# Three rounded passes for the scores and values of a memory attention, on pairs of token tiles

## What is computed

```python
def cross_attn(h, k, v, w_xq, w_xo):
    b, t, _ = h.shape
    q = (h @ w_xq).reshape(b, t, MEM_HEADS, MEM_HD)
    s = jnp.einsum('bthd,bmhd->bhtm', q, k).astype(jnp.float32) * (MEM_HD ** -0.5)
    p = jax.nn.softmax(s, axis=-1).astype(v.dtype)
    o = jnp.einsum('bhtm,bmhd->bthd', p, v).reshape(b, t, D_MODEL)
    return o @ w_xo
```

## Time and profile before

| | us |
|---|---|
| median of 3 runs | 2224.11 |
| lowest and highest run | 2221.91, 2224.35 |
| the profiled execution | 2224.57 |
| its span in the profile | 2222.8 |
| PE busy | 2191.7 |
| DVE busy | 1372.6 |
| ACT busy | 684.4 |

### The profile page before, as it was taken

How to read it: one execution, slowest core, us unless ns; L and a number is a source line. 1 busy time by engine, 2 the same in 40 slices (tenths; PEclk the granted TensorE clock), 3 DMA queues, 4 the chain that set the end, 5 groups by cost and what they waited for, 6 DMA issues and landing times.

```text
span 2222.8 us, 40929 instructions
## 1 busy us (share of the span) xinstructions
PE 2191.7 (99%) x15968; PEld 2137.3 (96%) x15968; DVE 1372.6 (62%) x2564; ACT 684.4 (31%) x1124; POOL 327.4 (15%) x335
## 2 busy tenths in 40 slices
PE   8999999999999999999999999999999999999998
PEld 7999999999999999987899988999999999999998
DVE  6865555646667765466868335258765555466665
ACT  6332232222123332246714034124323222221124
POOL 2010100123221000024400000000111010133230
PEclk9999999999999999999999999999999999999999
DMA  7231231243323221057623334422223123153222
GB/s 235 68 110 57 69 102 57 90 170 112 106 77 129 72 59 40 21 175 245 209 91 118 132 114 142 146 93 76 88 63 110 57 76 96 58 208 114 78 77 79
DMA packets 222577, 234.37 MB, mean 105 GB/s; under 512 B 8979, under 2 KB 179745, under 8 KB 222201
## 3 DMA queue, kind: packets, MB, share of 16 engines
q1 hardware_dynamic: 222465, 232.83, 32.3%
HBM read 180.42 MB, written 52.48 MB: 105 GB/s over the span
## 4 chain that ended last, share of the span: by engine, by line
PE 61%; DVE 2%; ACT 1%; DMA 1%; issue 0%; SPq 0%; DVEq 0%; ACTq 0%
PE bank L3018 18%; PE bank L3020 17%; PE bank L3019 17%; PE bank L3685 1%; PE bank L3697 1%; PE bank L3717 1%; PE bank L3578 0%; PE bank L3574 0%; PE bank L3584 0%; PE bank L3706 0%; PE bank L3739 0%; DMA w_raw<-in_w_out_dram 0%; DMA out_mem_k_prompt_dram<-kst 0%; PE bank L3727 0%; ACT dec L1658 0%
## 5 line engine op out<-in xcount | busy, mean ns | idle before, releaser
L3018 PE MATMUL bank<-h_hi,w_hi 128*128 128x352 f32 (+1 forms) x3392 | 1048.5, 309 | 1.7 <-DVE h_lo L2912 1.1
L3020 PE MATMUL bank<-h_hi,w_lo 128*128 128x352 f32 (+1 forms) x3392 | 1040.3, 307 | 0.0
L3019 PE MATMUL bank<-h_lo,w_hi 128*128 128x352 f32 (+1 forms) x3392 | 1040.0, 307 | 0.0
L3018 PEld LDWEIGHTS bank<-h_hi,w_hi 128*128 128x128 f32 x3392 | 636.8, 188 | 4.3 <-DVE h_lo L2912 1.4
L3019 PEld LDWEIGHTS bank<-h_lo,w_hi 128*128 128x128 f32 x3392 | 637.9, 188 | 0.0
L3020 PEld LDWEIGHTS bank<-h_hi,w_lo 128*128 128x128 f32 x3392 | 636.8, 188 | 0.0
L2208 DVE SCALAR_TENSOR_TENSOR x<-bank,x 128x352 f32<-128x352 f32 x448 | 226.8, 520 | 129.7 <-PE bank L3020 128.8
L3019 PE MATMUL bank<-xr,w_hi 128*128 128x264 f32 x640 | 181.8, 284 | 0.0
L3018 PE MATMUL bank<-xr,w_hi 128*128 128x264 f32 x640 | 181.4, 283 | 0.1
L3020 PE MATMUL bank<-xr,w_lo 128*128 128x264 f32 x640 | 181.5, 284 | 0.0
L1944 DVE TENSOR_TENSOR w_lo<-w_raw,w_hi 128x1024 fp32r<-128x1024 f32 x120 | 144.4, 1218 | 23.5 <-ACT w_hi L1264 23.5
(11 more groups left out here) (431 smaller groups left out, 2850.5 us busy)
## 6 DMA issues: line engine op xcount, KB each, us to landing
act_keep<-act SPq DMA_DIRECT2D x88, 264.0 KB, 2.0
w_raw<-in_w_gate_dram SPq DMA_DIRECT2D x44, 512.0 KB, 5.1
w_raw<-in_w_up_dram SPq DMA_DIRECT2D x44, 512.0 KB, 3.9
w_raw<-in_w_down_dram SPq DMA_DIRECT2D x44, 512.0 KB, 3.6
h_raw<-act_keep SPq DMA_DIRECT2D x24, 528.0 KB, 4.5
l_raw<-act_keep SPq DMA_DIRECT2D x20, 528.0 KB, 5.4
w_raw<-in_w_in_dram SPq DMA_DIRECT2D x18, 512.0 KB, 4.4
x<-x_keep SPq DMA_DIRECT2D x6, 1408.0 KB, 10.5
```

The source lines that it names most:

```text
L3018: eng.matmul(out, a_hi, b_hi, start=first, stop=False, skip_group_check=onto)
L3019: eng.matmul(out, a_hi, b_lo, start=False, stop=False, skip_group_check=onto)
L3020: return eng.matmul(out, a_lo, b_hi, start=False, stop=last, skip_group_check=onto)
```

## The change

In the attention, scores and values become three rounded passes, and an item becomes a **unit** u of one head and two token tiles (16 units; the heads of a pair of tiles come in the order 0, 3, 1, 2).

- **Splits.** ACT makes the high parts of `q` (into `h_hi`), of `kT` and of `v`, DVE the low parts: tiles 0 to 4 of `q`, `kT` and `v` around the last `evict_q`, tiles 5 to 7 in the units 2, 4 and 6. PE's first scores wait for the low part of `kT`.
- **Scores** of a unit: 2 tiles x 2 blocks x 3 passes of 256 columns, 12 matmuls in place of 8 exact ones. **Values**: 2 x 2 x 3 passes of 256 columns, 12 in place of 8 exact ones of 128 columns over 2 tiles.
- **Turned weights** of a unit fill bank 4 (512 columns): ACT takes the high part and DVE the low part (`att_turned`), where DVE made one copy.
- **Sample keys.** All four groups of sequence b stand in unit b. ACT copies groups 0, 1 and 2, DVE group 3 (`take_key`), as the last of its operations of the unit except a split; `sample_scores(b)` waits for it (`kt_copied`).
- **Sample values** come two to a unit, in units 11 to 14.
- **Weights.** The third and fourth unit of `w_xo` are split after the last values (the slots hold `kT_hi` and `v_hi` until then). `w_split(U_XO + 2)` stands on DVE between the last low part and the low part of the sample rows. The loads of units 4 and 5 of `w_xo` move behind the reload of `x`.

```diff
-            for group in range(2):
-                hi_pair(U_XQ + 4 + 4 * group)
-                hi_pair(U_XQ + 6 + 4 * group)
...
+            for pair in range(3):
+                hi_pair(U_XQ + 4 + 2 * pair)
...
+            for t in range(5):
+                q_hi(t)
+            eng.wait_ge(p_ready, 100)
+            eng.wait_ge(s_rows, 48)
+            eng.activation(kT_hi[:, :, :], kT[:, :, :], ACT.Copy).then_inc(n_hi, 1)
+            eng.activation(v_hi[:, :, :], v[:, :, :], ACT.Copy).then_inc(n_hi, 1)
...
+                if nq == 22:
+                    q_lo(4)
+                    row_lo("k", kT_lo, kT, kT_hi)
+            row_lo("v", v_lo, v, v_hi)
...
             att_exp(0)
+            att_turned(0)
             att_exp(1)
...
+            for u in range(NU):
+                if u < NB:
+                    take_key(u, 0)
+                    take_key(u, 1)
+                if u + 2 < NU:
+                    att_exp(u + 2)
+                if u >= 1:
+                    att_o(u - 1)
+                if u + 1 < NU:
+                    att_turned(u + 1)
+                if u < NB:
+                    take_key(u, 2)
+                if u in (2, 4, 6):
+                    q_hi(4 + u // 2)
...
+            for u in range(NU):
+                if u + 2 < NU:
+                    att_max(u + 2)
+                if u == S_SOFT:
+                    sample_max()
+                if u >= 1:
+                    att_lo(u - 1)
+                if u + 2 < NU:
+                    att_scale(u + 2)
+                if u + 1 < NU:
+                    att_turned(u + 1)
+                if u < NB:
+                    take_key(u)
...
+            att_lo(NU - 1)
+            w_split(U_XO + 2)
+            eng.wait_ge(a_oh, NU + 1)
...
+            w_split(U_XO + 3)
...
+                        mm = three(o, h_hi[:, a, tk], h_lo[:, a, tk], kT_hi[:, 2 * h + kd, :], kT_lo[:, 2 * h + kd, :],
+                                   kd == 0, kd == 1)
...
+                        mm = three(o, v_hi[:, m, c_:c_ + P], v_lo[:, m, c_:c_ + P], pT_hi[u % 2][:, m, :], pT_lo[u % 2][:, m, :],
+                                   m == 0, m == 1)
...
-                eng.wait_ge(b_ta, 4 * b + 4)
+                eng.wait_ge(b_ta, 3 * b + 3)
+                eng.wait_ge(kt_copied, 4 + b + 1)
...
+            for u in range(NU):
+                if u + 2 < NU:
+                    scores(u + 2)
+                if u < NB:
+                    sample_turn(u, 0)
+                    sample_turn(u, 1)
+                if u + 1 < NU:
+                    turn_p(u + 1)
+                if u < NB:
+                    sample_turn(u, 2)
+                    sample_turn(u, 3)
+                values(u)
+                if u < NB:
+                    sample_scores(u)
```

More of the change, by code:

```diff
@@ L448, in y_banks, with unit_at, split_done @@
             return (2 * (t % 2), 2 * (t % 2) + 1) if t < 7 else ((4, 5), (7, 6))[t - 7]
-        def turn_bank(i):
-            return bank[6 if i > 18 and i % 2 else 4]
+        def unit_at(u):
+            return u // MH, HEADS_AT[u % MH]
+        def split_done(what):
+            return N_SPLIT + SPLIT.index(what) + 1
         def down_bank(dl):
@@ L953, in _ @@
                 eng.dma_start(vring[b % 4][:, :, :], vc[:, b]).then_inc(s_in[b % 4], 16)
-            for k in range(4, 6):
-                unit(U_XO + k, wv["w_xo"][:, :, k * P:(k + 1) * P])
-            eng.wait_ge(a_o, 4 * NB)
+            eng.wait_ge(a_o, NU)
             eng.wait_ge(b_v, NB)
@@ L960, in _ @@
                 eng.dma_start(x[:, :, cols(n)], x_spill[:, :, cols(n)]).then_inc(s_back[n], 16)
-            for k in (6, 7):
+            for k in range(4, 8):
                 unit(U_XO + k, wv["w_xo"][:, :, k * P:(k + 1) * P])
@@ new lines, in att_turned, with att_o @@
+            def att_turned(u):
+                eng.wait_ge(a_t, u + 1)
+                wait(eng, a_o, u - 1)
+                eng.activation(pT_hi[u % 2], bank[4][:, :].rearrange("p (m t) -> p m t", m=2), ACT.Copy).then_inc(a_th, 1)
+            def att_o(u):
+                eng.wait_ge(a_o, u + 1)
+                tp, h = unit_at(u)
+                eng.activation(h_hi[:, 2 * h:2 * h + 2, 2 * tp * P:2 * (tp + 1) * P],
+                               bank[(2, 5)[u % 2]][:, :].rearrange("p (j t) -> p j t", j=2), ACT.Copy).then_inc(a_oh, 1)
@@ new lines, in att_exp, with take_key @@
+            def att_exp(u):
+                eng.wait_ge(a_m, u + 1)
+                wait(eng, a_t, u - 1)
+                for j in range(2):
+                    c_ = 2 * (u % 2) + j
+                    eng.activation(pr[c_][:, :], bank[u % 2][:, 256 * j:256 * j + 256], ACT.Exp, bias=amax[:, c_:c_ + 1],
+                                   scale=ATT_SCALE, accum_out=amax[:, 4 + c_:5 + c_]).then_inc(a_e, 1)
+            def take_key(b, g):
+                eng.wait_ge(b_t, 4 * b + g + 1)
+                if g == 0:
+                    wait(eng, b_s, b)
+                eng.activation(kTs[:, 2 * g:2 * g + 2, :].rearrange("p a b -> p (a b)"), bank[(3, 6)[g % 2]][:, :],
+                               ACT.Copy).then_inc(b_ta, 1)
@@ L2853, in add_out @@
                 eng.sem_inc(p_free, 1)
[L2855 to L2869, removed]
@@ L2884, in att_max @@
                 link(eng.tensor_scalar(m_, m_, -ATT_SCALE, None, ALU.mult))
                 eng.sem_inc(a_m, 1)
[L2887 to L2895, removed]
-            att_scale(0)
[L2897 to L2908, removed]
@@ L2909, in _, with att_scale, take_key @@
-            att_lo(NHT - 1)
-            eng.wait_ge(a_oh, 33)
+            def att_scale(u):
+                c_ = 2 * (u % 2)
+                eng.wait_ge(a_e, 2 * u + 2)
+                link(eng.reciprocal(amax[:, 12 + c_:14 + c_], amax[:, 4 + c_:6 + c_]))
+                for j in range(2):
+                    eng.tensor_scalar(pr[c_ + j][:, :], pr[c_ + j][:, :], amax[:, 12 + c_ + j:13 + c_ + j], None, ALU.mult)\
+                       .then_inc(a_n, 1)
+            def take_key(b):
+                eng.wait_ge(b_t, 4 * b + 4)
+                wait(eng, b_s, b)
+                eng.tensor_copy(kTs[:, 6:8, :].rearrange("p a b -> p (a b)"), bank[6][:, :]).then_inc(kt_copied, 1)
@@ L3689, in values, with scores @@
[L3689 to L3694, removed]
+            def scores(u):
+                tp, h = unit_at(u)
+                wait(eng, a_e, 2 * (u - 1))
+                eng.wait_ge(n_lo, split_done("k" if tp < 2 else "q5" if tp == 2 else "q7"))
+                for j in range(2):
+                    o, tk = bank[u % 2][:, 256 * j:256 * j + 256], slice((2 * tp + j) * P, (2 * tp + j + 1) * P)
+                    for kd in range(2):
+                        a = KT - 1 - 2 * h - kd
+                        mm = three(o, h_hi[:, a, tk], h_lo[:, a, tk], kT_hi[:, 2 * h + kd, :], kT_lo[:, 2 * h + kd, :],
+                                   kd == 0, kd == 1)
+                mm.then_inc(a_s, 1)
@@ new lines, in turn_p, with values @@
+            def turn_p(u):
+                eng.wait_ge(a_n, 2 * u + 2)
+                wait(eng, a_c, u)
+                for m in range(2):
+                    for j in range(2):
+                        c_ = 256 * m + P * j
+                        mm = eng.transpose(bank[4][:, c_:c_ + P], pr[2 * (u % 2) + j][:, m * P:(m + 1) * P], ident[:, :])
+                mm.then_inc(a_t, 1)
+            def values(u):
+                tp, h = unit_at(u)
+                eng.wait_ge(a_c, u + 1)
+                wait(eng, a_ol, u - 1)
+                if u == 0:
+                    eng.wait_ge(n_lo, split_done("v"))
+                for d_ in range(2):
+                    o, c_ = bank[(2, 5)[u % 2]][:, 256 * d_:256 * d_ + 256], (2 * h + d_) * P
@@ L3695, in values @@
                     for m in range(2):
-                        c_ = (2 * h + dt2) * P
-                        mm = eng.matmul(o, v[:, m, c_:c_ + P], pT[i % 2][:, m, :], start=(m == 0), stop=(m == 1))
+                        mm = three(o, v_hi[:, m, c_:c_ + P], v_lo[:, m, c_:c_ + P], pT_hi[u % 2][:, m, :], pT_lo[u % 2][:, m, :],
+                                   m == 0, m == 1)
                 mm.then_inc(a_o, 1)
[L3700 to L3706, removed]
-                                       pr[i % 2][:, m * P:(m + 1) * P], ident[:, :])
-                mm.then_inc(a_t, 1)
@@ L3742, in sample_values @@
                 mm.then_inc(b_v, 1)
[L3744 to L3747 removed]
+            scores(0)
+            scores(1)
             turn_p(0)
[L3749 to L3761 removed]
+            for u in range(NU):
[12 more added lines that the diff above has]
+                    sample_scores(u)
+                if u == S_BACK:
                     eng.wait_ge(b_d, 2)
```

163 lines of the change are left out of this document (85 added, 78 removed).

## The result

The changed kernel takes **2243.41 us** (median of 6 runs, 2241.95 to 2245.25) against 2224.06 us of the kernel before in the same runs (2221.91 to 2224.59): a ratio of 1.0089, 95% interval 1.0078 to 1.0099. It is 19 us slower. The profiled executions differ by 18.2 us (a span of 2241.0 against 2222.8). All of it lies in the attention: from the first sample scores to the output projection the kernel before needs 1400.91 - 1309.30 = 91.6 us, the changed one 1419.21 - 1309.94 = 109.3.

A forecast was written before the change was run, and what follows sets the result against it. PE bounded the kernel before; the change would make a closed chain over PE, ACT and DVE the bound. 1.2 + 10.5 - 2.3 + 2 = +11.4 us gave 2235.5 us, range 2227 to 2246.

The forecast's parts named there:

- its own case: Whole kernel: slower through a closed chain of waits in the attention, 2229 to 2241 us; chance 0.62.
- rival 1: Attention loop: the clock falls in every unit, 8 x 1.2 to 8 x 1.4 us, giving 2243 to 2245; chance 0.17.
- The clock: Attention units: PE's 2.2 us waits bring half clock, two falls allowed for, +2 us (0 to +9.6).
- PE's work: Attention unit with sample keys: PE needs 6.16 us, 0.118 per 256-column pass, 0.7 less than before.
- The ring: Attention's first half: a closed chain over PE, ACT and DVE takes 8.37 us a unit against 6.87, +10.5 us.
- The start: Up to the first sample scores: they come at 1310.5 instead of 1309.30, +1.2 us (0.4 to 2).
- The stretch behind the keys: From the last sample scores on: 41.2 us against 43.5 before, -2.3 us (-5 to +1).
- The grown end: After the last values: low part and w_xo split ahead of the sample rows make 3.2 us, 2.5 before.
- Two of the signs: Attention's first half: the wait view's first row is PE for DVE `kTs`; PE is about 74% busy.
- the Trainium skill's rule: TensorE's clock: brief idles between matmul groups cycling through PSUM banks can swing it between half and full; every unit would pay.

The follow-up runs named there:

- the reordered kernel: The changed kernel with operation orders on TensorE, ScalarE and VectorE and the w_xo split's place changed together, same arithmetic: 2213.05 us, ratio 0.9951 to the kernel before.
- the first experiment: The changed kernel with each unit's scores of u + 3 made an extra time, unused, ahead of the sample scores: 2235.99 us, ratio 1.0058 to the kernel before.

## Why the prediction was right, point by point

It gave 2235.5 us in a range of 2227 to 2246, slower at 0.82; measured were 2243.4. Direction, mechanism and range held; the middle was 8 us low. The measured time lies outside the 2229 to 2241 of its own case, which had a chance of 0.62; the range holds it only because it was drawn up to rival 1 (0.17). The clock accounts for 7.3 us of the 8; the other terms together were 0.4 too high, and 1.1 is that the medians differ by 19.3 us and the profiled executions by 18.2.

- **PE's work.** A pass of 256 columns is 0.118 from start to start, the value taken from 264 columns. The full unit in the reordered kernel is 6.27, 0.1 above the sum; in the changed kernel PE is busy for 6.39 of 8.41, 0.2 above it.
- **The ring.** 8.37 us by the sum, 8.41 in the trace without a fall; 7 x (8.41 - 6.87) = 10.8 us against 10.5. The wait on PE was put at 2.2 and is 2.02. The 512-column operations of DVE, unseen before, last 0.68 to 0.69. Taking away single links (key copy to ACT, high part first, scores early, a pass less) moved the period to 7.18, 7.34, 6.95 and 7.94, each within 0.15 of its sum: the ring is shown, not only argued.
- **The start.** +1.2 forecast, 1309.94 - 1309.30 = +0.6 measured; PE's projection ahead of it ran 0.5 us earlier in this trace (a query block on DVE at 1293.03, before 1293.51), so the step itself is about +1.1: from that block to the first sample scores are 16.9 us here and 15.8 before. Where the block stands differs from execution to execution (1295.40 in the trace of the experiment with the split behind the sample rows, which has the same instructions up to there, and again 16.9 us up to the first sample scores), so half a microsecond of this term is chance.
- **The stretch behind the keys.** 1419.21 - 1376.54 = 42.7 us with one fall of 1.5 in it, so 41.1 without, against 41.2 by the sum and 43.5 before. The trace of the first experiment has no fall there: up to the last turned weights it is 1.54 us shorter (32.66 against 34.20). The grown end was right too: 2.73 us of wait, with the split in it.
- **The clock: the step that was mis-sized.** It said two falls at 1.2 us, +2 us (0 to 9.6). There were six, at 9.95 - 8.41 = 1.54 us each: +9.3. The number was the larger mistake, four falls more at 1.2 us (4.8) against 0.34 us more for each of six (2.0). The prediction held the loop's own full clock at 16.73 busy of 19.10 us against it, and gave rival 1, a fall in every unit with 2243 to 2245 us, a chance of 0.17; of seven waits of 2.02 us six were followed by a fall. That rival 1 gives the measured time is partly luck: it has eight falls at 1.2 to 1.4 us, the trace six at 1.54. The row to go by was the mixer's 1.97 us wait, while the longest single wait in the stretch with 16.73 of 19.10 was 1.15 us, in the trace of the kernel before:

```profile
1363.97 0.41 PE L3706 MATMUL bank<-ident,pr 128*128 128x128 f32 x2 [1.15 <-DVE pr L2892]
```

The price was low because the slow stretches began with the work behind the wait and not within the wait (1318.86 behind 1318.35, at the latest 1349.6 behind 1348.20), so nearly all of the 1.7 us came onto the ring.

The terms with what was measured: 0.6 + 10.8 - 2.4 + 9.3 = 18.3 us, the 18.2 of the two spans.

Two of the signs came out otherwise. The wait view does not name DVE's copy of `kTs`; its first row says "issue":

```profile
PE bank L3823 <- issue: 15.2, 8, 2.0
```

And PE's busy share in the keys' stretch is 79% (52.49 of 66.30) and not 74%: a unit without a fall has 76% (6.39 of 8.41), and the slow stretches count as busy. For the Trainium skill's rule (TensorE: Matmul & The Clock Gate, A second HAM failure mode: psum-queue depth-cycling): here the trace agrees, the clock swings between 1.2 and 2.4 GHz with the idles between groups of matmuls, though the idle here is the wait for a copy of keys; it does so at 2.02 us, in six units of seven and not in each, and not in any unit at 0.6 to 0.94.

## What to carry to other kernels

Less work on the busiest engine is worth its time only while nothing around it becomes a closed chain: lay out, from the order, what one item hangs on and sum it from start to start, before counting the work. An operation that goes to a less loaded engine takes on every wait that stands ahead of it there; where it is due decides, not how full the engine is. And when TensorE must wait, put useful work of the next item into the wait first: here 1.42 us of even useless matmuls per unit gave back 7 us, by keeping the clock up.

## What the runs showed of the hardware

- A wait of 2.02 us of TensorE once in 8.4 us was followed by a granted clock of 0.50 (1.2 GHz) for 3.4 us in six cases of seven; with waits of 0.60, 0.61, 0.79 and 0.93 us in units of 7 to 8.4 us it did not fall in any of the eight units. A longer wait in shorter units (2.3 to 2.5 us in 7.94) brought four falls in seven: it does not go by the wait's length alone, and what else it goes by stays open here. The wait of 2.7 us ahead of the output projection had a fall at it in four of the six traces that have such a wait. The wait of 2.1 us ahead of the first turned weights had one in one trace of the seven that have it.
- A fall cost 1.52 to 1.58 us in the changed kernel, where the work behind the wait is on the chain, and 1.3 to 1.5 with two passes, where less of it is; at half clock a 256-column pass takes 0.213 us from start to start, at full clock 0.118.
- A pass in the rounded type takes 0.118 us for 256 columns, where one exact matmul takes 2 x 0.216: three passes are 0.35 against 0.43. The scores of a unit were four exact matmuls before (eight records, 1.73 us), and not eight as the section on the change has it; the values were eight of 128 columns (2 x 0.89 = 1.78 us). Twelve passes take 1.42 us in place of either; that the values had twice 128 columns made a difference of only 0.05 us.
